# Scatter of the experts' results: two fp32r products with a 0-or-1 selection, the gate in VectorE's sum, and the next expert's turn between the two scatters

## Chip, core and metric

The kernel runs on one core of a Trainium2 chip. The metric is the device time in microseconds (us) of one execution. Three runs of the kernel before gave 2854.1 to 2858.06 us with a median of 2854.6.

## The reference

Two blocks of one model and two of another are computed one after the other for 256 tokens of 1024 features, all in fp32. The change touches only the mixture of experts in the second block. Eight experts exist, each token goes to two of them, and an expert is a SwiGLU with 3584 hidden columns:

```python
def _moe(x, w_router, w1, w3, w2):
    ...
    logits = (xt @ w_router).astype(jnp.float32)
    top_v, top_e = lax.top_k(logits, TOP_K)
    gates = jax.nn.softmax(top_v, axis=-1)
    ...
    def run(args):
        xb, e = args
        return _swiglu(xb, w1[e], w3[e], w2[e])
    yb = lax.map(run, (buf.reshape(n_blocks, EXPERT_BLOCK, D), block_e)).reshape(P, D)
    y = jnp.zeros((T, D), x.dtype).at[stok].add(yb[dest] * sg[:, None].astype(x.dtype))
```

The last line is the scatter: each expert's rows go back to their tokens, times the gate, and are summed.

## The kernel before, in words

**Products.** A weight product in fp32 accuracy is made from three fp32r products: each factor is split into a high and a low part, and `mm3` (lines L689, L690, L691) adds high x high, low x high and high x low. Weights come in units of 1 MB (4 x 128 rows by 512 columns). SyncE loads a unit into one of 5 `raw` buffers, ScalarE rounds it to `whi` (L1311), VectorE subtracts to `wlo` (L1717), both with 3 buffers, and TensorE takes 12 products from a unit of an expert. `Plan` writes one order of steps, and every engine walks through it (`Engine.run`). At each step an engine first prepares the weights of the units up to two ahead (`step` and `ahead`, `AHEAD = 2`), and then does its part of the step. So ScalarE and VectorE make the weights of unit u + 2 ahead of the evacuation of unit u's product, each in its own program order.

**An expert.** `select` (VectorE) makes from each token's place in the expert a matrix `sel` of 0 and 1 in fp32r, and `selg`, the same times the gate, in fp32. `gather` multiplies `sel` with the rows of x to give the expert's inputs `xT`, high and low. `turn` transposes `selg` on TensorE (L1005), and ScalarE copies it to `selgT` (L1411). Seven column blocks of e1 and e3 follow (28 units), each made into the hidden `hb` and transposed (`across`, L1015) into `hTe`. Then e2 runs in two column blocks of seven units. ScalarE copies each result to `hb` (L1522), and `scatter` multiplies `selgT` by it in fp32 (L1025). A plain fp32 product of 128x512 shows as two records in the trace. VectorE adds the result to `y` (L1830; for the very last one L2129, ahead of LayerNorm). Both scatters of an expert stand behind its last e2 unit, for the last expert the first one stands after three units of the second block.

**The branch.** The tokens of an expert fill one or two tiles of 128. The program holds both versions. `Engine.expert` reads the count and branches (L549: `If(self.count[ex] > 128)`), on TensorE, ScalarE and VectorE each. In these inputs every expert has one tile, so the second arm runs. TensorE does some things ahead of the branch: the `turn`, and nine products (three mm3) of the first unit (`open_expert`, L961). The branch stands behind them in its program. On ScalarE and VectorE the branch comes right after the last step of the expert before.

**Waits.** The sequencer of an engine takes instructions in order, and one that has to wait for a semaphore holds all behind it. Four PSUM buffers are given out in turn (`fill`), and each is free when its evacuation has been counted.

Of the kernel before, what the change touches and what calls it, by code (L numbers as in the profile page):

```python
# [70 lines left out]
class Memory:  # L71
# [21 lines left out]

    def new(self, name, shape, dt, c, side):
        self.serial += 1
        return c.enter_context(self.nc.sbuf_tensor(f"{name}_{self.serial}", shape, dt, side=side))
# [67 lines left out]
    def moe(self, t, hl, c):  # L164
        self.y1 = t("y", [128, 2, 1024], F32, c)
        with ExitStack() as c0:
# [10 lines left out]
            self.sel, self.selg = t("sel", [128, 2, 256], F32R, c0), t("selg", [128, 2, 256], F32, c0)  # L177
            self.selgT = t("selgT", [128, 2, 256], F32, c0)
# [72 lines left out]
class Plan:  # L251
# [128 lines left out]
    def moe(self):  # L380
        a, m, o = self.a, self.m, self.order
        for ex in range(8):
# [3 lines left out]
            o += [("begin", ex), ("turn", ex)]  # L386
# [14 lines left out]
            o += e2[0][ex == 7:] + e2[1][0:n] + [("scatter", ex, 0)] + e2[1][n:] + [("scatter", ex, 1), ("finish", ex)]  # L401
# [165 lines left out]
class Tensor(Engine):  # L567
# [25 lines left out]
    def do(self, step):  # L593
# [60 lines left out]
        elif what == "gather":  # L654
            self.gather(*a)
        elif what == "across":
# [297 lines left out]
    def expert(self, ex, j0, j1):  # L954

        self.turn(ex)
# [42 lines left out]
    def turn(self, ex):  # L999
        e, m = self.e, self.m  # L1000
        ps = self.fill(("turn", ex), ("selgT", ex))
        for s in range(2):
            for q in range(2):
                o = s * 256 + q * 128
                ins = e.transpose(ps[:, o:o + 128], m.selg[:, q, s * 128:s * 128 + 128], m.ident[:, :])  # L1005
# [12 lines left out]
    def scatter(self, ex, cb):  # L1018
        e, m = self.e, self.m
        ps = self.fill(("sc", ex, cb), ("y", ex, cb))  # L1020
        e.wait_ge(*self.at("selgT", ex))
        e.wait_ge(*self.at("ev", "e2", ex, cb))
        for q in range(2):
            for s in range(self.tiles):
                ins = e.matmul(ps[:, q * 512:q * 512 + 512], m.selgT[:, s, q * 128:q * 128 + 128], m.hb[:, cb, s, :],  # L1025
                               start=(s == 0), stop=(s == self.tiles - 1))
# [275 lines left out]
class Scalar(Engine):  # L1302
# [25 lines left out]
    def do(self, step):  # L1328
# [80 lines left out]
        elif what == "turn":  # L1409
            e.wait_ge(*self.at("full", "turn", a[0]))  # L1410
            e.activation(m.selgT[:, :, :], bands(self.psum("turn", a[0]), 4)[:, 0:2, :], ACT.Copy) \  # L1411
                .then_inc(*self.up("a_moe", ("selgT", a[0])))
        elif what == "across":
# [4 lines left out]
                .then_inc(*self.up("a_moe", ("hiT", "hTe", ex, cb)))  # L1418
        elif what == "rms":
# [45 lines left out]
    def product(self, g, G):  # L1465
# [47 lines left out]
        elif nm == "e1":  # L1513
# [3 lines left out]
            elif ex:  # L1517
                e.wait_ge(*self.at("full", "sc", ex - 1, cb))
# [183 lines left out]

    def copy(self, full, key, dst, o, n, parts=0):
# [6 lines left out]
class Vector(Engine):  # L1710
# [26 lines left out]
    def do(self, step):  # L1737
# [88 lines left out]
        elif what == "scatter" and a != (7, 1):  # L1826
# [3 lines left out]
            e.tensor_tensor(yy, yy, bands(self.psum("sc", *a)), ALU.add).then_inc(*self.up("d_moe", ("y",) + a))  # L1830
# [1072 lines left out]
```

## Time and profile before

| | |
|---|---|
| runs | 2854.6 us median, 2854.1 to 2858.06 |
| the profiled execution, its own time | 2857.58 us |
| its span, first to last instruction | 2855.5 us |
| mean granted TensorE clock | 0.986 of full speed |
| TensorE busy | 2743.5 us, 96% |
| VectorE busy | 2111.4 us, 74% |
| ScalarE busy | 1629.1 us, 57% |
| weight splitting on VectorE (L1717) | 1304.2 us in 588 instructions |

Engines are named PE (TensorE's products), PEld (its weight loads), DVE (VectorE), ACT (ScalarE), POOL and SP; a name with q is the engine's sequencer. Matmul records overlap, since a product is issued before the one ahead of it is through: the distance between two starts is what one costs in a row of them. The experts' stage lasts from about 845 to 1890 us of the span.

### The profile page before, as it was taken

How to read it: one execution, taken by the hardware profiler on the slowest of the kernel's cores; microseconds unless marked ns; L12 is line 12 of the kernel's file. 1: busy time of each engine (PE TensorE's matmuls, PEld its weight loads, DVE VectorE, ACT ScalarE, POOL GpSimd, SP SyncE). 2: the span in 40 equal slices, each digit the busy share in tenths (PEclk: the TensorE clock that was granted, in tenths of full speed). 3: DMA queues.
4: the chain of work that ended last, by engine and by line, in shares of the span. 5: the costliest groups of instructions: out<-in, count | busy, mean ns of one | idle time of the engine just before them, and what ended most of it. 6: DMA issues, size and time to landing. Idle time of an engine off the chain costs nothing.

```text
span 2855.5 us, 44738 instructions
## 1 busy us (share of the span) xinstructions
PE 2743.5 (96%) x19124; PEld 2324.9 (81%) x19124; DVE 2111.4 (74%) x2115; ACT 1629.1 (57%) x1630; POOL 140.4 (5%) x152
## 2 busy tenths in 40 slices
PE   7989999998999999999999999999899999998999
PEld 7867899887778787878788787878678988877997
DVE  6657655646769898988889898977756876766685
ACT  4345443454547676767667676755554654554563
POOL 1000000000000000000000000000330000052000
PEclk9999999999999999999999999999999999999999
DMA  7344655554349999999999999973205555322552
GB/s 215 118 134 139 194 188 172 150 169 152 122 163 350 322 357 332 340 350 338 343 346 340 324 355 347 361 238 130 79 30 174 178 192 168 124 70 69 175 181 104
DMA packets 360334, 616.16 MB, mean 216 GB/s; under 512 B 13776, under 2 KB 117200, under 8 KB 360112
## 3 DMA queue, kind: packets, MB, share of 16 engines
q1 hardware_dynamic: 355216, 598.61, 59.9%
q0 software_dynamic: 4896, 14.36, 2.2%
q8 instruction: 168, 2.75, 0.4%
q14 instruction: 54, 0.44, 0.0%
HBM read 611.88 MB, written 1.05 MB: 215 GB/s over the span
## 4 chain that ended last, share of the span: by engine, by line
PE 84%; DVE 8%; ACT 5%; issue 2%; DMA 0%; SPq 0%; DVEq 0%; ACTq 0%
PE ps L689 24%; PE ps L691 24%; PE ps L690 24%; ACT whi L1311 2%; DVE wlo L1717 2%; PE ps L1025 1%; PE ps L994 1%; PE ps L1171 1%; PE ps L1015 1%; PE ps L1150 1%; PE ps L1182 1%; PE ps L810 1%; ACT Q L1682 0%; PE ps L834 0%; ACT W L1706 0%
## 5 line engine op out<-in xcount | busy, mean ns | idle before, releaser
L1717 DVE TENSOR_TENSOR wlo<-raw,whi 128x2048 fp32r<-128x2048 f32 (+2 forms) x588 | 1304.2, 2223 | 426.0 <-ACT whi L1311 418.4
L1311 ACT ACTIVATE whi<-raw 128x2048 fp32r<-128x2048 f32 (+2 forms) x588 | 1092.9, 1860 | 422.9 <-PE ps L691 404.3
L689 PE MATMUL ps<-whi,xTh 128*128 128x512 f32 (+4 forms) x1464 | 582.4, 398 | 13.2 <-issue 5.9
L690 PE MATMUL ps<-wlo,xTh 128*128 128x512 f32 (+4 forms) x1464 | 571.4, 390 | 0.0
L691 PE MATMUL ps<-whi,xTl 128*128 128x512 f32 (+4 forms) x1464 | 570.7, 390 | 0.0
L689 PE MATMUL ps<-xTh,whi 128*128 128x256 f32 x1480 | 419.3, 283 | 0.0
L691 PE MATMUL ps<-xTh,wlo 128*128 128x256 f32 x1480 | 418.0, 282 | 0.0
L690 PE MATMUL ps<-xTl,whi 128*128 128x256 f32 x1480 | 418.0, 282 | 0.0
L689 PEld LDWEIGHTS ps<-whi,xTh 128*128 128x128 f32 x1464 | 280.7, 192 | 79.2 <-issue 13.5
L691 PEld LDWEIGHTS ps<-whi,xTl 128*128 128x128 f32 x1464 | 280.6, 192 | 62.1
L690 PEld LDWEIGHTS ps<-wlo,xTh 128*128 128x128 f32 x1464 | 281.2, 192 | 56.6
L689 PEld LDWEIGHTS ps<-xTh,whi 128*128 128x128 f32 x1480 | 279.7, 189 | 0.8 <-issue 0.7
L690 PEld LDWEIGHTS ps<-xTl,whi 128*128 128x128 f32 x1480 | 279.7, 189 | 0.1
L691 PEld LDWEIGHTS ps<-xTh,wlo 128*128 128x128 f32 x1480 | 279.5, 189 | 0.0
L689 PE MATMUL ps<-whi,hTeh 128*128 128x512 f32 x448 | 178.7, 399 | 0.0
L690 PE MATMUL ps<-wlo,hTeh 128*128 128x512 f32 x448 | 177.6, 396 | 0.0
L691 PE MATMUL ps<-whi,hTel 128*128 128x512 f32 x448 | 177.6, 396 | 0.0
L691 PEld LDWEIGHTS ps<-whi,hTel 128*128 128x128 f32 x448 | 84.4, 188 | 20.6
L689 PEld LDWEIGHTS ps<-whi,hTeh 128*128 128x128 f32 x448 | 84.4, 188 | 20.4 <-issue 0.2
L690 PEld LDWEIGHTS ps<-wlo,hTeh 128*128 128x128 f32 x448 | 84.4, 188 | 20.3 <-issue 0.2
L2584 DVE SCALAR_TENSOR_TENSOR co<-ci,cwf,co 128x256 f32<-128x256 f32 x176 | 73.8, 480 | 0.9
L689 PE MATMUL ps<-whi,hT2h 128*128 128x512 f32 x176 | 69.4, 395 | 0.0
(557 smaller groups left out, 3492.7 us busy)
## 6 DMA issues: line engine op xcount, KB each, us to landing
raw<-in_expert_w_dram SPq DMA_DIRECT2D x336, 1024.0 KB, 5.7
raw<-in_w_in_dram SPq DMA_DIRECT2D x76, 1024.0 KB, 5.1
raw<-in_w_up_dram SPq DMA_DIRECT2D x44, 1024.0 KB, 5.1
raw<-in_dense_w_dram SPq DMA_DIRECT2D x32, 1024.0 KB, 5.2
raw<-in_w_down_dram SPq DMA_DIRECT2D x20, 1024.0 KB, 5.4
raw<-in_w_out_dram SPq DMA_DIRECT2D x16, 1024.0 KB, 5.0
raw<-in_w_branch_diff_dram SPq DMA_DIRECT2D x8, 1024.0 KB, 5.0
raw<-in_w_ple_gate_dram SPq DMA_DIRECT2D x8, 1024.0 KB, 5.0
```

What stands on the lines that cost most here:

```text
L689: self.e.matmul(out, ah, bh, start=start, stop=False)
L690: self.e.matmul(out, ah, bl, start=False, stop=False)
L691: return self.e.matmul(out, al, bh, start=False, stop=stop)
L810: ins = self.e.transpose(ps[:, o:o + 128], src[:, t, (k0 + k) * 128:(k0 + k + 1) * 128], self.m.ident[:, :])
L994: ins = e.matmul(ps[:, d * 256:d * 256 + 256], m.xs[half][:, q, (d0 + d) * 128:(d0 + d + 1) * 128], m.sel[:, q, :], start=(q == 0), stop=( ...
L1015: ins = e.transpose(ps[:, o:o + 128], m.hb[:, cb % 2, t, k * 128:k * 128 + 128], m.ident[:, :])
L1025: ins = e.matmul(ps[:, q * 512:q * 512 + 512], m.selgT[:, s, q * 128:q * 128 + 128], m.hb[:, cb, s, :], start=(s == 0), stop=(s == self.ti ...
L1150: ins = self.e.transpose(out(r_), src[:, 128 * r_:128 * r_ + 128], self.m.ident[:, :])
L1171: ins = e.matmul(ps[half(a_), span(512 * c + 64 * r_)], m.E[d][r, s], TT[r, s], start=True, stop=True)
L1311: self.e.activation(self.m.hi[u % NHL][:, 0:n], self.m.raw[u % NRAW][:, 0:n], ACT.Copy) \
L1717: self.e.tensor_tensor(self.m.lo[u % NHL][:, 0:n], self.m.raw[u % NRAW][:, 0:n], self.m.hi[u % NHL][:, 0:n].bitcast(F32), ALU.subtract) \
L2584: ins = e.scalar_tensor_tensor(co[k][:, c, :], ci[:, c, tap:tap + 256], wc, co[k][:, c, :], ALU.mult, ALU.add)
```

## The change

`select` no longer makes `selg`. The turn now transposes `sel` itself, and the result is kept as `selT` in fp32r in two buffers, one expert apart. The results of e2 are split: ScalarE writes a high half (`expert_high`) and VectorE a low half (`expert_low`) in fp32r, into the part of `hTe` that e2 has read by then (`expert_sum`), no longer into `hb`. The scatter is then two fp32r products for each token tile, `selT` by high and `selT` by low. The gate is applied by VectorE when it adds to `y`. The halves of the first column block are made in a step of their own, `rest`, after two units of the second block. The turn of expert ex + 1 leaves `Tensor.expert` and becomes a step between the two scatters of expert ex; the one of expert 0 comes ahead of its `begin`, and the last expert has none behind it.

```diff
-            self.sel, self.selg = t("sel", [128, 2, 256], F32R, c0), t("selg", [128, 2, 256], F32, c0)
-            self.selgT = t("selgT", [128, 2, 256], F32, c0)
+            self.sel = t("sel", [128, 2, 256], F32R, c0)
+            self.selT = [t(f"selT{k}", [128, 2, 256], F32R, c0) for k in range(2)]
...
+    def expert_sum(self, cb):
+
+        return [h[:, 4 * cb:4 * cb + 4, :].rearrange("p (t a) n -> p t (a n)", t=2) for h in self.hTe]
...
-            o += [("begin", ex), ("turn", ex)]
+            o += [("turn", 0)] if ex == 0 else []
+            o += [("begin", ex)]
...
-            o += e2[0][ex == 7:] + e2[1][0:n] + [("scatter", ex, 0)] + e2[1][n:] + [("scatter", ex, 1), ("finish", ex)]
+            o += e2[0][ex == 7:] + e2[1][0:2] + [("rest", ex, 0)] + e2[1][2:n] + [("scatter", ex, 0)] + e2[1][n:]
+            o += [("turn", ex + 1)] if ex < 7 else []
+            o += [("scatter", ex, 1), ("finish", ex)]
...
     def expert(self, ex, j0, j1):
 
-        self.turn(ex)
         self.opened = ("e1", ex, 0)
...
     def turn(self, ex):
         e, m = self.e, self.m
-        ps = self.fill(("turn", ex), ("selgT", ex))
+        e.wait_ge(*self.at("sel", ex))
+        ps = self.fill(("turn", ex), ("selT", ex))
...
     def scatter(self, ex, cb):
         e, m = self.e, self.m
-        ps = self.fill(("sc", ex, cb), ("y", ex, cb))
-        e.wait_ge(*self.at("selgT", ex))
+        ps, T = self.fill(("sc", ex, cb), ("y", ex, cb)), m.selT[ex % 2]
+        high, low = m.expert_sum(cb)
+        e.wait_ge(*self.at("selT", ex))
+        e.wait_ge(*self.at("hiT", "ev", "e2", ex, cb))
+        for q in range(2):
+            for s in range(self.tiles):
+                e.matmul(ps[:, q * 512:q * 512 + 512], T[:, s, q * 128:q * 128 + 128], high[:, s, :], start=(s == 0), stop=False)
         e.wait_ge(*self.at("ev", "e2", ex, cb))
         for q in range(2):
             for s in range(self.tiles):
-                ins = e.matmul(ps[:, q * 512:q * 512 + 512], m.selgT[:, s, q * 128:q * 128 + 128], m.hb[:, cb, s, :],
-                               start=(s == 0), stop=(s == self.tiles - 1))
+                ins = e.matmul(ps[:, q * 512:q * 512 + 512], T[:, s, q * 128:q * 128 + 128], low[:, s, :], start=False,
+                               stop=(s == self.tiles - 1))
...
+        elif what == "rest":
+            e.wait_ge(*self.at("unit", self.p.unit[("e2", a[0], 1), 0]))
+            self.expert_high(*a)
...
         elif nm == "e2":
-            e.activation(m.hb[:, g[2], 0:self.tiles, :], bands(ps)[:, 0:self.tiles, :], ACT.Copy) \
-                .then_inc(*self.up("a_moe", ("ev",) + g))
+            if g[2]:
+                self.expert_high(*g[1:])
...
+    def expert_high(self, ex, cb):
+        g, n = ("e2", ex, cb), self.tiles
+        self.e.wait_ge(*self.at("full", *g))
+        self.e.activation(self.m.expert_sum(cb)[0][:, 0:n, :], bands(self.psum(*g))[:, 0:n, :], ACT.Copy) \
+            .then_inc(*self.up("a_moe", ("hiT", "ev") + g))
...
-            e.tensor_tensor(yy, yy, bands(self.psum("sc", *a)), ALU.add).then_inc(*self.up("d_moe", ("y",) + a))
+            for t in range(2):
+                ins = e.scalar_tensor_tensor(yy[:, t, :], bands(self.psum("sc", *a))[:, t, :], m.gate[:, t, a[0]:a[0] + 1],
+                                             yy[:, t, :], ALU.mult, ALU.add)
+            ins.then_inc(*self.up("d_moe", ("y",) + a))
...
+    def expert_low(self, ex, cb):
+        g, n, (high, low) = ("e2", ex, cb), self.tiles, self.m.expert_sum(cb)
+        self.e.wait_ge(*self.at("hiT", "ev", *g))
+        self.e.tensor_tensor(low[:, 0:n, :], bands(self.psum(*g))[:, 0:n, :], high[:, 0:n, :].bitcast(F32), ALU.subtract) \
+            .then_inc(*self.up("d_moe", ("ev",) + g))
...
         for t in range(2):
-            e.tensor_scalar(m.selg[:, t, :], m.iota[:, :], m.pos[:, t, ex:ex + 1], m.gate[:, t, ex:ex + 1], ALU.is_equal,
-                            ALU.mult)
             ins = e.tensor_scalar(m.sel[:, t, :], m.iota[:, :], m.pos[:, t, ex:ex + 1], m.mask[:, t, ex:ex + 1],
                                   ALU.is_equal, ALU.mult)
```

VectorE calls `expert_low` where ScalarE calls `expert_high`: in the step `rest`, and after the last unit of e2's second block. ScalarE's sigmoid of e1 waits for a transposition of the expert before instead of its scatter, and its copy of selT from expert 2 on also for the second scatter of two experts before.

## Rows read from the trace of the kernel before

**Rows 1.** The page, busy time of the engines.
```profile
PE 2743.5 (96%) x19124; PEld 2324.9 (81%) x19124; DVE 2111.4 (74%) x2115; ACT 1629.1 (57%) x1630; POOL 140.4 (5%) x152
```
**Rows 2.** Busy time by engine, from the scatter of one expert to the next.
```profile
core 0: us, PE busy (x) PEld busy (x) DVE busy (x) ACT busy (x) POOL busy (x), PEclk, DMA share, GB/s
1107.80:1236.70 128.90, 128.90 (x577) 103.36 (x576) 114.19 (x72) 91.00 (x61) 0.00 (x0) 1.00 0.96 343
```
**Rows 3.** Timeline of PE at the joint of the first two experts.
```profile
start us, us, engine line op out<-in xcount [idle before <-releaser]
...
977.43 3.60 PE L1025 MATMUL ps<-hb,selgT 128*128 128x512 f32 x8
980.87 0.60 PE L1005 MATMUL ps<-ident,selg 128*128 128x128 f32 x4
...
981.54 0.40 PE L690 MATMUL ps<-wlo,xTh 128*128 128x512 f32 x1
981.77 0.40 PE L691 MATMUL ps<-whi,xTl 128*128 128x512 f32 x1
...
984.89 0.50 PE L689 MATMUL ps<-whi,xTh 128*128 128x512 f32 x1 [1.31 <-issue]
```
**Rows 4.** Line L549 in the whole span: duration ns min/median/max, first and last start.
```profile
L549 PEldq COMPARE_BRANCH  x8: 3442/4606/5910, 851.0 to 1756.4; - x8
```
**Rows 5.** Lines L549 and L1022 at the joints of 977.43 and 1236.72.
```profile
L1022 PEldq EVENT_SEMAPHORE  x1: 51/51/51, 978.3 to 978.3; - x1
...
L549 PEldq COMPARE_BRANCH  x1: 5907/5907/5907, 978.9 to 978.9; - x1
...
L549 PEldq COMPARE_BRANCH  x1: 4438/4438/4438, 1238.0 to 1238.0; - x1
```
**Rows 6.** Timeline of PE at the joint of 1236.72.
```profile
1236.72 3.60 PE L1025 MATMUL ps<-hb,selgT 128*128 128x512 f32 x8
...
1242.70 0.39 PE L689 MATMUL ps<-whi,xTh 128*128 128x512 f32 x1
```
**Rows 7.** Waits of the experts' stage: us in total, times, longest.
```profile
PE ps L689 <- issue: 4.9, 4, 1.3
```
**Rows 8.** DMA within the branch, first of 978.9, then of 851.0.
```profile
q1 hardware_dynamic: 841, 1.66, 81.1%
q8 instruction: 2, 0.03, 4.0%
...
DMA packets 1, 0.02 MB, mean 5 GB/s; under 512 B 0, under 2 KB 0, under 8 KB 0
```
**Rows 9.** Timeline of ACT at the joint of 977.43.
```profile
977.63 0.60 ACT L1522 ACTIVATE hb<-ps 128x512 f32<-128x512 f32 x1 [0.84 <-PE ps L691]
```
**Rows 10.** Groups of VectorE and ScalarE by form in the experts' stage: busy, mean ns.
```profile
L1724 DVE TENSOR_TENSOR hTel<-ps,hTeh 128x512 fp32r<-128x512 f32 x56 | 38.2, 681 | 0.0
...
L1417 ACT ACTIVATE hTeh<-ps 128x512 fp32r<-128x512 f32 x56 | 33.3, 594 | 10.6 <-PE ps L1015 10.6
```
**Rows 11.** Timeline of DVE at the first joint, and at the last expert's end.
```profile
976.83 2.29 DVE L1717 TENSOR_TENSOR wlo<-raw,whi 128x2048 fp32r<-128x2048 f32 x1 [0.52 <-ACT whi L1311]
...
1881.18 2.29 DVE L1717 TENSOR_TENSOR wlo<-raw,whi 128x2048 fp32r<-128x2048 f32 x1 [0.51 <-ACT whi L1311]
```
**Rows 12.** Timeline of DVE ahead of the first expert.
```profile
848.39 2.35 DVE L1818 CAST xTl<-ps 128x1024 fp32r<-128x1024 f32 x2
```
**Rows 13.** Busy time in stretches with and behind idle times of PE.
```profile
536.80:538.60 1.80, 0.02 (x2) 0.04 (x1) 1.76 (x4) 0.01 (x1) 0.00 (x0) 1.00 0.00 0
539.80:543.10 3.30, 3.21 (x11) 3.19 (x11) 3.21 (x4) 1.71 (x3) 2.80 (x6) 0.50 0.71 114
984.90:990.00 5.10, 5.10 (x22) 4.13 (x23) 3.43 (x2) 3.21 (x3) 0.00 (x0) 1.00 0.57 192
2031.40:2038.10 6.70, 6.70 (x40) 4.51 (x40) 2.76 (x7) 4.06 (x9) 4.24 (x4) 0.50 0.67 241
```
**Rows 14.** Timeline of PE at the end of the last expert.
```profile
1882.72 1.96 PE L1025 MATMUL ps<-hb,selgT 128*128 128x512 f32 x4 [0.78 <-ACT hb L1522]
1884.51 10.46 PE L834 MATMUL ps<-ident 128*128 128x512 f32 x24
```

More of the change, by code:

```diff
@@ L655, in do @@
             self.gather(*a)
+        elif what == "turn":
+            self.turn(*a)
         elif what == "across":
@@ L1004, in turn @@
                 o = s * 256 + q * 128
-                ins = e.transpose(ps[:, o:o + 128], m.selg[:, q, s * 128:s * 128 + 128], m.ident[:, :])
+                ins = e.transpose(ps[:, o:o + 128], m.sel[:, q, s * 128:s * 128 + 128].bitcast(F32), m.ident[:, :])
         ins.then_inc(*self.up("turned_moe", ("full", "turn", ex)))
@@ L1410, in do @@
             e.wait_ge(*self.at("full", "turn", a[0]))
-            e.activation(m.selgT[:, :, :], bands(self.psum("turn", a[0]), 4)[:, 0:2, :], ACT.Copy) \
-                .then_inc(*self.up("a_moe", ("selgT", a[0])))
+            if a[0] > 1:
+                e.wait_ge(*self.at("full", "sc", a[0] - 2, 1))
+            e.activation(m.selT[a[0] % 2][:, :, :], bands(self.psum("turn", a[0]), 4)[:, 0:2, :], ACT.Copy) \
+                .then_inc(*self.up("a_moe", ("selT", a[0])))
         elif what == "across":
@@ L1517, in product @@
             elif ex:
-                e.wait_ge(*self.at("full", "sc", ex - 1, cb))
+                e.wait_ge(*self.at("full", "ac", ex - 1, 6 - cb))
             e.activation(m.hb[:, cb % 2, 0:self.tiles, :], bands(ps)[:, 0:self.tiles, :], ACT.Sigmoid) \
@@ L1829, in do @@
             e.wait_ge(*self.at("full", "sc", *a))
-            e.tensor_tensor(yy, yy, bands(self.psum("sc", *a)), ALU.add).then_inc(*self.up("d_moe", ("y",) + a))
+            for t in range(2):
+                ins = e.scalar_tensor_tensor(yy[:, t, :], bands(self.psum("sc", *a))[:, t, :], m.gate[:, t, a[0]:a[0] + 1],
+                                             yy[:, t, :], ALU.mult, ALU.add)
+            ins.then_inc(*self.up("d_moe", ("y",) + a))
+        elif what == "rest":
+            e.wait_ge(*self.at("unit", self.p.unit[("e2", a[0], 1), 0]))
+            self.expert_low(*a)
         elif what == "rms":
@@ L2128, in layernorm @@
                 e.wait_ge(*self.at("full", "sc", 7, 1, t))
-                e.tensor_tensor(yy, yy, bands(self.psum("sc", 7, 1))[:, t, :], ALU.add).then_inc(*self.up("d_moe", ("y", 7, 1)))
+                e.scalar_tensor_tensor(yy, bands(self.psum("sc", 7, 1))[:, t, :], m.gate[:, t, 7:8], yy, ALU.mult, ALU.add) \
+                    .then_inc(*self.up("d_moe", ("y", 7, 1)))
             e.wait_ge(*self.prev)
@@ L2181, in product @@
             return
-        if nm in ("q", "k", "v", "cq", "ck", "uq", "ukv", "pp", "rt", "e2", "dc", "gm", "qa", "ka"):
+        if nm in ("q", "k", "v", "cq", "ck", "uq", "ukv", "pp", "rt", "dc", "gm", "qa", "ka"):
             return
@@ L2256, in product @@
             return
+        elif nm == "e2":
+            if g[2]:
+                self.expert_low(*g[1:])
         elif nm == "oat":
```

## The prediction

> **What bounds the kernel now.** I read the page first. TensorE is busy for 96% of the span, VectorE for 74% [rows 1]. A change that takes work from TensorE could pay in full, unless that work covers something else. So I looked next at one expert. From the scatter of one to the scatter of the next are 128.9 us, all of it TensorE work at a granted clock of 1.00, with VectorE busy for 114 us and ScalarE for 91 [rows 2]. No product inside an expert waits for weights. The place that matters is the joint between two experts.
>
> In the timeline of a joint the scatter begins at 977.43. I call this moment t0. The eight records of the two fp32 scatters last to 980.87, 0.43 us each; four transposes (the turn) follow, then nine opening products of the next expert to about 983.4, and the tenth starts only at 984.89, after 1.31 us of idle time put down to "issue" [rows 3]. It waits for no engine. In program order the `If` of `Engine.expert` (L549) lies between the ninth product and the tenth. The row of L549 says what it costs TensorE's sequencer: 3.44 to 5.91 us, eight times [rows 4]. At this joint it starts at 978.9 and takes 5.9 us, so it ends at 984.8, and TensorE goes on at 984.89. At the joint of 1236.72 it takes 4.44 us from 1238.0, ends just as the nine products are spent, and the tenth follows at 1242.70 without a break [rows 5, 6]. So the sequencer runs ahead of the array and starts the branch while the scatter still runs; scatter, turn and nine products are its cover. Of the seven joints four have a branch of 4.4 to 4.6 us and resume at about t0 + 6.0; three have 5.8 to 5.9 us and resume at t0 + 7.2 to 7.5. These three and the first expert's are the four idle times of 4.9 us in sum in the stage's waits [rows 7]. The mean is t0 + 6.6. Within the branch the instruction queue reads 16 KB once or twice, next to a weight queue at 81% [rows 8]: the branch jumps over the arm for two tiles.
>
> The Trainium skill, page "Runtime: NRT & Kernel Launch", section "Instruction fetch mechanics", says that a taken branch whose target is outside a window of two pages must fetch the target page by DMA before execution can go on. The reads inside the branch agree with it. The page "Advanced Engine Details and Errata", section "Control Flow Timing", gives about 108 ns for a compare-and-branch. TensorE's 3.4 to 5.9 us disagree; by that figure the joints would be bound by the array alone, which is the third rival's case.
>
> What starts the branch? The sequencer passes its wait ahead of the second scatter (L1022) at 978.3 [rows 5], right after ScalarE's copy of the second e2 product ends (977.63 + 0.60) [rows 9]. The branch follows 0.6 us later. So it is this evacuation that sets its start, at t0 + 1.4 on the average, not the array.
>
> **The change part by part.**
>
> *The products.* A scatter with one tile is two fp32 products, each two records of 0.43 us. It becomes four fp32r products; the nearest row, fp32r with 512 columns, is issued 0.235 us after the one before [rows 3]. Two scatters fall from 3.44 to 1.88 us: 1.55 us of array time for each expert, 12.4 for eight.
>
> *The second scatter's wait.* It waited for one ScalarE copy. Now ScalarE writes the high half (0.59 us, as L1417) and then VectorE the low half (0.68, as L1724, the same size and types) [rows 10]. VectorE takes its steps in order, and its step for the last e2 unit begins with the low weights of the unit two ahead, the wlo of 976.83, which ends at 979.12 [rows 11]. The low half can only follow: ready at about 979.75, t0 + 2.3. The first scatter and the turn are over at t0 + 1.3, the second's high products at 1.8; then the array waits for some 0.6 us. Behind this wait stand two low products, the next expert's waits, nine opening products and the branch. The first expert shows this case: VectorE's xTl ended at about 850.75, the branch behind nine products started at 851.0 [rows 4, 12]. Between that 0.3 us and the 0.6 above I take 0.4: the branch starts at t0 + 2.7 instead of t0 + 1.4. The turn, moved forward, takes its four transposes out of the way from wait to branch, and its place in the cover with it.
>
> *Where TensorE resumes.* The array's own work would be done at t0 + 5.0 (2.4 + 0.47 + 2.1). The branch ends at 2.7 + its length, and 0.05 later work goes on. The median length of 4.6 gives t0 + 7.35, the mean of the seven, 5.1, gives 7.85; the shortest, 3.44, gives 6.2, the longest 8.65. I take 4.8, since the weight transfers that share the queues are a little nearer to their end: t0 + 7.55 against 6.6. That is 0.95 us later, seven times: +6.7. The ends are -0.4 and +2.05 each, so -3 and +14.
>
> *The clock.* An idle time of about 2.4 us now stands at each joint, with 0.6 us shortly before it. An idle time of 1.8 us was followed by a granted clock of 0.50 (1.2 instead of 2.4 GHz) for over 3 us; the joint's 1.3 us was followed by 1.00 [rows 3, 13]. The work in 3.4 us at half the clock costs 1.7 us more. I take four of the seven joints: +6.8. The bounds are 0 and, since a stretch of 6.7 us at 0.50 is in the rows too, 7 x 3.4 = 24.
>
> *The halves for cb 0 ("rest")* are made inside e2's second product. ScalarE idles for 0.8 to 0.9 us and VectorE for 0.5 ahead of each weight unit there [rows 9, 11], so 0.59 fits, and 0.68 makes one wlo 0.2 us late; the weights are prepared a unit ahead. Nothing; without that cover 0.2 x 8 = 1.6.
>
> *The rest of VectorE and ScalarE.* `select` loses two of its four instructions, the sum becomes two instructions of 512 columns for one of 1024, the low halves add 2 x 0.68: at most 1.4 us for an expert, on an engine that has 15 to spare [rows 2]. Nothing. After the joint, its next wlo would be ready at about t0 + 7.3 (sums to 5.0, then 2.29) and is needed some 3.5 us after TensorE resumes. selT is copied earlier than selgT was. Expert 0's turn stays where it was.
>
> *The last expert.* Its first scatter lies between weight units with no branch behind: four records go from 0.43 to 0.235 us, -0.8. Its second waited 0.78 us for ScalarE. Now the low half follows the wlo of 1881.18 (to 1883.45) [rows 11], is ready at 1884.1, and its products end at 1884.6, where the filler records began at 1884.51 before [rows 14]: +0.1. LayerNorm's chain on VectorE comes 0.7 us later, which these fillers (10.5 us, and nothing idle behind them) hide; else +0.7.
>
> *Sum*: 6.7 + 6.8 - 0.8 + 0.1 = +12.8. The profiled execution took 2857.58 us (span 2855.5), 3.0 above the median of the runs, 2854.6. On its own time that is 2870.4, on the median 2867.4.
>
> **Rivals.** *First: late branch, but the clock is kept, and branches are mostly short.* Then +4 to +8, less 0.7: 2858 to 2862. For it: a gap of 1.3 us left the clock alone. Against it: 2.4 is longer than the 1.8 that didn't.
>
> *Second: the branch is as quick as at the first expert*, where TensorE waited for VectorE right ahead of it too: 6.2 against 6.6, seven times, less 0.7: -3.5, 2851. Against it: one packet moved in that branch, the instruction read alone, while at a joint two weight loads are under way [rows 8].
>
> *Third, on the other side: the branch ends inside its cover.* It decides if the branch takes less than 2.3 us (5.0 less 2.7). The joint then goes from 6.6 to 5.0: 7 x -1.6 less 0.7 = -12, 2843. For it: twelve microseconds of array time do go, and TensorE is the busiest engine. Against it: the shortest of eight branches took 3.44.
>
> *Fourth: everything at its worst*, branches of 5.9 us and the clock down at each joint, twice as long at some: 14 + 12 to 24, 2880 to 2892. For it: three of seven were that long.
>
> VectorE as the bound has no chance of its own (115 of 129 us), and that fp32r saves nothing is excluded by its pitch.
>
> **How the numbers follow.** Forecast (2862 to 2877) 0.48; first rival 0.20; second 0.12; third 0.10; fourth 0.10. About 0.2%, 5.7 us, is what a measurement of this kernel can tell from no change. Faster beyond it: the third rival and a little of the second, 0.11. Slower: forecast, fourth, and nearly half of the first, 0.67. Same: 0.22. The range for 8 in 10 runs from 2851 to 2880; it leaves out the third and the fourth.
>
> **What would show it.** Right: the scatter's records 0.235 us apart; a wait of the second scatter's low products for VectorE until about t0 + 2.4; L549 on TensorE starting at t0 + 2.7 with 4 to 6 us; TensorE idle for 2 to 3.5 us behind the nine opening products, put down to "issue"; PEclk 0.50 behind several joints. Wrong: a low half ready by t0 + 1.5, ahead of the wlo; a branch of 2 us; or a branch that starts before the second scatter's wait is passed.

## The result, and the profile after

The change makes the kernel slower: 2887.86 us (median of four runs, 2881.13 to 2890.96) against 2855.63 us (2854.1 to 2858.06), a ratio of 1.0107 (95% interval 1.0094 to 1.0121). The direction and the place were forecast, the size was not: +32 us, where the forecast was +12.8 and its range ended at 2880. The profiled execution took 2886.58 us, 29.0 more than that of before.

The page of the kernel after, first the busy times that answer to [rows 1], then a line of its costliest groups. The last figures of that line are the idle time ahead of it and what ended it:
```profile
span 2884.5 us, 44791 instructions
...
PE 2746.4 (95%) x19124; PEld 2333.6 (81%) x19124; DVE 2121.5 (74%) x2130; ACT 1629.3 (56%) x1630; POOL 141.3 (5%) x152
...
L698 PE MATMUL ps<-whi,xTh 128*128 128x512 f32 (+4 forms) x1464 | 587.8, 402 | 33.6 <-issue 26.1
```
The span is 29 us longer and TensorE is busy for only 3 us more. The rest is idle time ahead of the first product of an `mm3` (L698, which was L689), and "issue" says that no engine released it. The waits of the experts' stage (850 to 1900 us), which answer to [rows 7]:
```profile
PE ps L698 <- issue: 25.1, 8, 3.6
PE ps L1039 <- DVE hTel L2301: 2.3, 7, 0.3
```
4.9 us of "issue" have become 25.1. The second scatter's wait for its low half is there at all seven joints with 0.3 us each.

Timeline of TensorE at the first joint, beside [rows 3]. L1035 is the scatter's high product, L1039 its low one, L1014 the turn:
```profile
977.64 0.63 PE L1035 MATMUL ps<-hTeh,selT 128*128 128x512 f32 x2
978.11 0.64 PE L1039 MATMUL ps<-hTel,selT 128*128 128x512 f32 x2
978.58 0.60 PE L1014 MATMUL ps<-ident,sel 128*128 128x128 f32 x4
978.94 0.71 PE L1035 MATMUL ps<-hTeh,selT 128*128 128x512 f32 x2
979.99 0.73 PE L1039 MATMUL ps<-hTel,selT 128*128 128x512 f32 x2 [0.34 <-DVE hTel L2301]
980.56 0.40 PE L698 MATMUL ps<-whi,xTh 128*128 128x512 f32 x1
...
982.43 0.40 PE L700 MATMUL ps<-whi,xTl 128*128 128x512 f32 x1
986.08 0.50 PE L698 MATMUL ps<-whi,xTh 128*128 128x512 f32 x1 [3.25 <-issue]
```
t0 is 977.64. The scatters are cheap as forecast, and the nine opening products are spent at 982.83. Then the array stands for 3.25 us. VectorE and ScalarE in the same stretch, beside [rows 9, 11], and the branch on TensorE's sequencer, L556 now, there and in the whole span, beside [rows 4, 5]:
```profile
977.04 2.29 DVE L1742 TENSOR_TENSOR wlo<-raw,whi 128x2048 fp32r<-128x2048 f32 x1 [0.52 <-ACT whi L1325]
979.25 0.68 DVE L2301 TENSOR_TENSOR hTel<-ps,hTeh 128x512 fp32r<-128x512 f32 x1
979.97 2.85 DVE L1856 SCALAR_TENSOR_TENSOR y<-ps,gate,y 128x512 f32<-128x512 f32 x4
```
```profile
977.90 0.60 ACT L1725 ACTIVATE hTeh<-ps 128x512 fp32r<-128x512 f32 x1 [0.90 <-PE ps L700]
```
```profile
L556 PEldq COMPARE_BRANCH  x1: 5674/5674/5674, 980.4 to 980.4; - x1
...
L556 PEldq COMPARE_BRANCH  x8: 3353/5820/6032, 851.3 to 1778.7; - x8
```
ScalarE has the high half at 978.50, but VectorE is in the wlo until 979.33, so the low half is ready at 979.93 and the branch starts at 980.4, t0 + 2.7. It is also longer: the median is 5.82 us, where [rows 4] had 4.61. Its end, 986.04, is where TensorE resumes.

What the branch waits for is seen in the queues. First SP's issue of a 1 MB weight load, before and after, then the DMA of the branch's first three microseconds (980.4 to 983.4) and of the rest (983.5 to 986; queue, kind: packets, MB, share):
```profile
979.15 0.37 SPq L2787 DMA_DIRECT2D raw<-in_expert_w_dram  x1
...
979.36 0.37 SPq L2826 DMA_DIRECT2D raw<-in_expert_w_dram  x1
```
```profile
DMA packets 546, 1.09 MB, mean 364 GB/s; under 512 B 16, under 2 KB 16, under 8 KB 545
q1 hardware_dynamic: 545, 1.08, 102.5%
q14 instruction: 1, 0.01, 0.6%
...
q1 hardware_dynamic: 59, 0.09, 9.4%
q8 instruction: 1, 0.02, 2.6%
```
The weights fill the DMA engines for three microseconds, and only then, at 983.55, comes q8, the read of 16 KB of instructions. The load was issued when the wlo of 977.04 was done, since that is what frees its buffer: 0.99 us ahead of the branch. In both kernels it comes at t0 + 1.72. It has not moved; the branch has moved from 0.2 to 0.4 us ahead of it to 1.0 us behind it. One read of 8 KB on the other instruction queue, q14, starts at 980.86, between the packets of two loads. By what rule the DMA engines serve their queues no run shows; what follows is about the times alone.

Last, busy time within the idle stretch, behind it, and over a mean period from this scatter on, beside [rows 2, 13] (PE, PEld, DVE, ACT, POOL, then PEclk, DMA share, GB/s):
```profile
982.90:986.00 3.10, 0.00 (x0) 0.00 (x0) 2.12 (x1) 0.00 (x0) 0.00 (x0) 1.00 0.31 114
987.00:990.00 3.00, 3.00 (x9) 2.32 (x8) 0.78 (x1) 1.91 (x1) 0.00 (x0) 0.50 0.83 315
...
977.64:1110.70 133.06, 129.47 (x578) 104.58 (x577) 115.44 (x74) 91.01 (x61) 0.00 (x0) 0.99 0.92 332
```
The stall comes at full clock, and 3.4 us at half of it follow, at every one of the seven joints. Taken from both traces, in us from t0 (means of the seven joints; the period, from one t0 to the next, is a mean of six):

| | before | after |
|---|---|---|
| branch starts | +1.3 to +1.5 | +2.70 to +2.74 |
| branch takes | 5.09 (4.41 to 5.91) | 5.83 (5.67 to 6.03) |
| instruction read starts, from the branch's start | 1.6 to 2.2, once 3.3 | 3.2 to 3.6 |
| TensorE resumes (start of the tenth product) | +6.58 | +8.60 |
| half clock behind it | none | 3.4 us, seven times |
| period | 129.60 | 133.06 |

So the seven joints cost 7 x 2.02 = 14.1 us of later resuming and 7 x (3.46 - 2.02) = 10.1 us of clock. The second figure is what is left of the longer period once the later resuming is taken off. With 0.6 us gained at the last expert and 0.2 lost ahead of the first joint that makes 23.8 of the 24.4 us by which the experts' stage grew.

### The profile page after: what moved, and what is told of

Read it like the earlier page. It is cut to its first block, busy times and chain, and to the rows that moved or that the text cites. A ratio compares the mean times of both kernels' runs of the same rounds, so it can differ in the third digit from the quotient of the medians.

```text
span 2884.5 us, 44791 instructions
## 1 busy us (share of the span) xinstructions
PE 2746.4 (95%) x19124; PEld 2333.6 (81%) x19124; DVE 2121.5 (74%) x2130; ACT 1629.3 (56%) x1630; POOL 141.3 (5%) x152
## 3 DMA queue, kind: packets, MB, share of 16 engines
HBM read 611.88 MB, written 1.05 MB: 212 GB/s over the span
## 4 chain that ended last, share of the span: by engine, by line
PE 82%; DVE 9%; ACT 6%; issue 3%; DMA 0%; DVEq 0%; SPq 0%; ACTq 0%
PE ps L698 24%; PE ps L700 24%; PE ps L699 23%; DVE wlo L1742 2%; ACT whi L1325 2%; PE ps L1002 1%; PE ps L1185 1%; PE ps L1024 1%; PE ps L1164 1%; PE ps L1196 1%; PE ps L819 1%; PE ps L843 0%; PE ps L932 0%; DMA raw<-in_w_in_dram 0%; ACT s L1621 0%
## 5 line engine op out<-in xcount | busy, mean ns | idle before, releaser
L698 PE MATMUL ps<-whi,xTh 128*128 128x512 f32 (+4 forms) x1464 | 587.8, 402 | 33.6 <-issue 26.1
L698 PE MATMUL ps<-xTh,whi 128*128 128x256 f32 x1480 | 418.9, 283 | 0.0
L698 PEld LDWEIGHTS ps<-whi,xTh 128*128 128x128 f32 x1464 | 284.4, 194 | 100.9 <-issue 34.2
L698 PEld LDWEIGHTS ps<-xTh,whi 128*128 128x128 f32 x1480 | 280.1, 189 | 0.8 <-issue 0.7
L698 PE MATMUL ps<-whi,hTeh 128*128 128x512 f32 x448 | 178.3, 398 | 0.0
L698 PEld LDWEIGHTS ps<-whi,hTeh 128*128 128x128 f32 x448 | 84.4, 188 | 20.2
L700 PE MATMUL ps<-whi,hT2l 128*128 128x512 f32 x176 | 69.5, 395 | 0.0
```

The source lines that it names most:

```text
L698: self.e.matmul(out, ah, bh, start=start, stop=False)
L700: return self.e.matmul(out, al, bh, start=False, stop=stop)
```

## The experiments

Two theories stood against each other at first. **The branch's cover**: everything is lost at the branch, because its start moved behind VectorE's wlo and its instruction read comes only behind the weight load that the same wlo releases. **The rest of the edit**: the split of e2's results, the sums, the turn's new place or the queues of ScalarE and VectorE cost something of their own. Each ratio is to the kernel before on the same chip; its medians there were 2856.5, 2857.2, 2857.3 and 2855.0 us for the four groups of runs below.

### No branch at all

Both kernels with only the arm for one tile, in all the engines that have it. What is left out is the arm for two tiles, which these inputs don't use.
```diff
-        with self.e.If(self.count[ex] > 128):
-            ...
-        with self.e.Else():
-            self.tiles = 1
-            for j in range(j0, j1):
-                self.step(j)
+        self.tiles = 1
+        for j in range(j0, j1):
+            self.step(j)
```


> The changed kernel without the branch: only the arm for one tile is in the program, which all eight experts of these inputs take; an expert of more than 128 tokens would be computed wrongly. Theory (the joint is bound by the branch, which starts late, and by the clock lost behind it): the tenth opening product follows the ninth without a break, resume at t0 + 5.0, no stretch at half clock in the experts' stage, expert period 133.1 -> about 129.1 us (the wait of 0.34 us for the low half stays), total 2887 -> about 2850. Rival (the halves, the sums or the weight pipeline cost the time): the period stays above 131 and the total above 2870.

> The kernel before without the branch, one-tile arm alone (it leaves out the arm for two tiles). Theory: the three joints that resume at t0 + 7.2 to 7.5 come down to 6.0, so -4 to -5 us in all, about 2850.5, period 128.8 everywhere. Against the changed kernel without the branch this gives what the fp32r scatter is worth by itself: 1.55 less 0.34 of waiting for the low half for each of seven joints, 0.8 in the last expert, so some 8 to 10 us if the array is the bound in both, and about 0 if fp32r saves nothing.

**Measured**: the kernel after takes 2844.96 us, ratio 0.9956 (0.9939 to 0.9972); the kernel before 2855.44, ratio 0.9995 (0.9983 to 1.0007). One period of each, after and then before:
```profile
1106.80:1234.60 127.80, 127.46 (x577) 103.33 (x577) 115.12 (x74) 91.00 (x61) 0.00 (x0) 1.00 0.97 345
```
```profile
1102.50:1231.30 128.80, 128.80 (x578) 103.46 (x577) 114.22 (x72) 90.98 (x61) 0.00 (x0) 1.00 0.95 342
```
Without the branch the edit does what it is made for: 1.0 us for each expert. From the first joint's t0 to the end of the last scatter the traces show 894.8 us against 902.1, so 7.4 less. The medians differ by 10.5, which their two intervals (together some 6 us either way) don't tell from that. The array's part of the prediction holds: 1.55 us less 0.58 of delay by the low half at each of seven joints, and 0.6 at the last expert, make 7.4. Both expected totals were missed. The kernel after came out 5 us below its 2850, with a period of 127.8 us where 129.1 was expected. The kernel before was to gain 4 to 5 us and shows no gain beyond its interval, though all its periods are 128.8 as expected. All that the kernel after loses, it loses at the branch: 2887.86 against 2844.96.

### The late copy alone

The kernel before, in which VectorE instead of ScalarE copies e2's second result, for experts 0 to 6. Nothing else of the change is in it.
```diff
         elif nm == "e2":
+            if g[2] and g[1] < 7: return                          # ScalarE
...
+        if nm == "e2" and g[2] and g[1] < 7:                      # VectorE
+            e.wait_ge(*self.at("full", *g))
+            e.tensor_copy(m.hb[:, 1, 0:self.tiles, :], ...).then_inc(...)
```


> The kernel before with one edit: VectorE instead of ScalarE copies e2's second result at the seven joints, so that it comes behind the wlo of the unit two ahead; products, gate and turn stay. Theory: the branch starts at t0 + 2.7 to 2.9 instead of 1.35, its instruction read falls behind the weight load issued at t0 + 1.7, it takes 5.7 to 6.0 us at all seven joints, TensorE resumes at t0 + 8.5 to 8.8 and the clock falls to 0.50 behind most joints (the array has 2.4 us more work after the wait here, so perhaps not behind all): 2869 to 2881. Rival (the branch's length was set by something else in the change, such as ScalarE's earlier branch): the branch starts late but takes 4.4 to 4.8 at most joints, resume at 7.3, +5 us, 2860.

**Measured**: 2883.34 us (2871.3 to 2891.12), ratio 1.0087 (1.0058 to 1.0116). VectorE and TensorE at the third joint:
```profile
1247.18 2.29 DVE L1719 TENSOR_TENSOR wlo<-raw,whi 128x2048 fp32r<-128x2048 f32 x1 [0.52 <-ACT whi L1311]
1249.39 0.68 DVE L2186 COPY hb<-ps 128x512 f32<-128x512 f32 x1
```
```profile
1250.22 1.95 PE L1025 MATMUL ps<-hb,selgT 128*128 128x512 f32 x4 [0.56 <-DVE hb L2186]
...
1256.39 0.51 PE L689 MATMUL ps<-whi,xTh 128*128 128x512 f32 x1 [1.67 <-issue]
```
```profile
L549 PEldq COMPARE_BRANCH  x1: 5627/5627/5627, 1250.7 to 1250.7; - x1
...
L549 PEldq COMPARE_BRANCH  x8: 3517/5875/7567, 853.7 to 1784.4; - x8
```
The copy stands behind the wlo, the branch starts at t0 + 2.8 to 3.0 and takes 5.6 to 6.2 us, at two joints with a second read 7.2 and 7.6. TensorE resumes at t0 + 8.6 to 10.6, and the half clock follows at five of seven joints. The median lies 2 us above the 2869 to 2881 expected. This one edit, without the new products, the gate in the sum or the moved turn, costs nearly what the whole change does.

### The whole change, but the load held back

The kernel after; SyncE waits with the load that the wlo releases until VectorE has added the second scatter, which is after the branch's start. The branch starts as late as before.
```diff
+            for ex in range(7):
+                if u == p.unit[("e2", ex, 1), 6] + 2 + NRAW:
+                    e.wait_ge(*self.at("y", ex, 1))
```


> The changed kernel with one wait more: at each joint SyncE issues the weight load that it issued at t0 + 1.7 only after the sum of the second scatter, at about t0 + 5.2. Theory (the instruction read of the branch stands in line behind that load): the branch still starts at t0 + 2.7 but takes 3.4 to 4.5 us, resume at t0 + 6.1 to 7.2, clock lost at half of the joints at most, total 2887 -> 2855 to 2868. Rival (the read is late for another reason, for example until the array has run dry): the branch keeps its 5.7 to 6.0 us and the total its 2887, or gets worse by the late load.

**Measured**: 2860.52 us (2853.69 to 2867.73), ratio 1.0009 (0.9999 to 1.002). The branch at the first joint and in the whole span, and the opening at that joint:
```profile
L556 PEldq COMPARE_BRANCH  x1: 3423/3423/3423, 983.5 to 983.5; - x1
...
L556 PEldq COMPARE_BRANCH  x8: 3407/3608/5114, 854.3 to 1763.2; - x8
```
```profile
983.16 0.74 PE L1039 MATMUL ps<-hTel,selT 128*128 128x512 f32 x2 [0.34 <-DVE hTel L2301]
...
987.00 0.50 PE L698 MATMUL ps<-whi,xTh 128*128 128x512 f32 x1 [1.01 <-issue]
```
The wait for the low half is the same 0.34 us and the branch starts at t0 + 2.70 as in the kernel after, but it takes 3.4 to 3.9 us instead of 5.7 to 6.0 (5.1 where two reads fall in it), TensorE idles for 1.0 to 1.5 us (2.7 at that one joint), and five of six periods are 129.1 to 129.5. Of what stands ahead of the branch only the load has moved. So the late start alone costs little; what costs is that it falls behind the load. The sixth period, 133.5 us, has a half clock of 6.8 us in it.

### Low half first

The kernel after; in the step of the last e2 unit VectorE makes the low half before the wlo instead of behind it.
```diff
+    def step(self, j):                                            # class Vector
+        s = self.p.order[j]
+        if s[0] == "u" and s[1][0] == "e2" and s[1][2] == 1 and s[2] == 6:
+            self.do(s)
+            self.j = j
+            self.ahead(min(self.p.end[j] + AHEAD, len(self.p.units)))
```


> The changed kernel with one turn of order: in the step of e2's last unit VectorE makes the low half first and the wlo of the unit two ahead after it. Theory: low half ready at t0 + 1.55, branch from t0 + 1.95, and the weight load that follows that wlo is issued at t0 + 3.9 instead of 1.7, behind the instruction read; the branch takes 3.4 to 4.6 us, resume at t0 + 5.4 to 6.6 against 6.55 before, clock kept; period 128 to 129.3, total 2850 to 2857. Rival (the weights made later at the joint cost what the earlier branch brings): TensorE waits for wlo behind the joint, total above 2860.

**Measured**: 2857.48 us (2854.0 to 2861.86), ratio 1.0001 (0.9991 to 1.0011).
```profile
L556 PEldq COMPARE_BRANCH  x8: 3347/3834/3966, 855.0 to 1756.1; - x8
```
The branch starts at t0 + 2.0, 3.1 us behind a load, and takes 3.6 to 4.0 us; TensorE resumes at t0 + 5.7 to 6.0, no half clock follows, and the periods are 128.6 to 128.9. The order of two VectorE instructions takes back the whole 30 us. From the first joint's t0 to the end of the last scatter it takes 900.9 us, where the kernel before takes 907.1 and the kernel after 931.2. And yet the total is the same as before. In its trace the stretch ahead of the first joint took 981.4 us against 977.4, with 6.8 us more at half clock, and the one behind the last scatter 977.5 against 970.9, with a wait of 1.5 us for VectorE (L836) that is new. These two stretches hardly differ between the programs, but over the fourteen traces of this document they lie between 972.8 and 981.4, and between 970.9 and 977.5. So a single trace can't say what takes the gain back, and it was not tried.

### A longer opening

The kernel after with 18 opening products instead of nine ahead of the branch, as cover.
```diff
-        for k in range(3):
-            self.mm3(...)
+        for j in range(2):
+            if j:
+                self.e.wait_ge(*self.at("lo", u + 1))
+            for k in range(3):
+                self.mm3(...)                                     # three of each unit
```


> The changed kernel with 18 opening products ahead of the branch instead of 9 (the first three k of the first two units). Theory: the branch starts at t0 + 2.8 to 3.0 and still takes 5.7 to 6.0 us, so it ends at 8.6 to 8.9, but the array works until t0 + 7.1 and has nine products less behind it; idle 1.5 us, which leaves the clock at 1.00; period about 129.7, total 2853 to 2862. It tells the two parts of the loss apart: 2.1 us of idle time and 1.4 us of clock for each joint. Rival: if the branch waited for the array to run dry it would now end at about t0 + 11 and the total would stay at 2885.

**Measured**: 2872.83 us (2867.05 to 2877.13), ratio 1.0056 (1.0034 to 1.0077). That is 15 us better than the kernel after, but the expected total was missed.
```profile
PE ps L698 <- issue: 16.1, 7, 6.9
PE ps L698 <- DVE wlo L1747: 4.4, 5, 0.9
...
L556 PEldq COMPARE_BRANCH  x8: 3338/5678/7312, 846.7 to 1766.5; - x8
```
The branch is as long as in the kernel after (5.6 to 6.2), so TensorE still resumes at t0 + 8.6 to 9.2. Nine more products, taken from behind the branch, cut the stall from 3.4 to 1.4 us at most joints, but 0.9 us come back at four of them, some 14 us behind t0. There TensorE waits for the fourth unit's wlo: the last three products of the first unit stand behind the branch now, and they free the buffers for it. At one joint two reads fall in the branch, it takes 7.3 us, and TensorE resumes only at t0 + 14.2. That is the 6.9 us of the first row. The branch explains 3 of them, and behind it the next 16 KB are read, 4.5 us after the load ahead of that read. Half clock follows at three joints.

### The rest of the edit

The kernel after, with e2's results in `hb`, no step `rest` and the scatter in fp32 as before, but with the 0-or-1 `selT` (in fp32), the gate in VectorE's sum and the turn between the scatters:
```diff
-            self.expert_high(*g[1:])
+            e.activation(m.hb[:, g[2], 0:self.tiles, :], ..., ACT.Copy).then_inc(...)
...
-   matmul(..., T, high, ...); matmul(..., T, low, ...)
+   matmul(..., T, m.hb[:, cb, s, :], ...)                        # fp32
```


> The changed kernel with the scatter put back to one fp32 product of ScalarE's copy in hb: the 0-or-1 selection, the gate in VectorE's sum and the turn between the scatters stay, the halves and the step rest go. Theory (these parts are harmless): branch from t0 + 1.35 with 4.4 to 5.9 us, same as the kernel before within 4 us, 2852 to 2860. Rival (the moved turn, or ScalarE's later branch behind it, does the harm): above 2865.

The kernel after with only the turn put back behind the second scatter:
```diff
-            o += [("turn", ex + 1)] if ex < 7 else []
             o += [("scatter", ex, 1)]
+            o += [("turn", ex + 1)] if ex < 7 else []
```


> The changed kernel with the turn behind both scatters again. Theory (the low half's wait starts the branch): it still starts at t0 + 2.7 to 2.8 and takes 5.7 to 6.0 us; the turn's 0.35 us moves into the cover where the array idles anyway, TensorE waits 0.35 longer for the low half, resume unchanged at t0 + 8.6, idle time a little shorter (3.3 instead of 3.65); total 2880 to 2888, as the changed kernel. Rival (the moved turn delays the branch or its read): the branch starts before t0 + 2.5 and the total falls by over 5 us.

**Measured**: with the fp32 scatter 2858.07 us, ratio 1.0004 (0.9994 to 1.0014); with the turn last 2885.73 us, ratio 1.0102 (1.0084 to 1.0121).
```profile
L556 PEldq COMPARE_BRANCH  x8: 3658/4496/6032, 849.0 to 1750.0; - x8
```
```profile
L557 PEldq COMPARE_BRANCH  x8: 3371/6004/6232, 846.7 to 1775.1; - x8
```
In the first the branch starts at t0 + 1.3 again, since ScalarE alone stands behind the second scatter, and it takes 4.3 to 4.8 us at six joints (6.0 at the seventh, where the read starts late). The gate in the sum, the selection and the moved turn are harmless. In the second the branch starts 0.1 to 0.2 us later than in the kernel after and takes 5.5 to 6.2 us, and TensorE idles for up to 0.6 us ahead of the low half's products instead of 0.34. So the place of the turn makes next to no difference.

### The load held back in the kernel before

The edit of SyncE above in the kernel before, where the wlo and so the load come behind the branch's start anyway.

> The kernel before with the weight load at each joint issued after the second sum (about t0 + 5) instead of t0 + 1.7. Theory (the read shares the queues with the loads in flight): the branch starts at t0 + 1.35 and takes 3.4 to 4.4 us at all joints, ending inside its cover; period 128.8, 4 to 5 us less in all, as without the branch: the same within noise or just faster. Rival (the two lengths 4.4 and 5.8 come from two instruction reads at once, not from the weight load): three joints still take 5.8 and resume at 7.2 to 7.5.

**Measured**: 2859.73 us (2854.86 to 2866.56), ratio 1.0017 (1.0006 to 1.0028).
```profile
L549 PEldq COMPARE_BRANCH  x8: 3670/4490/6075, 846.2 to 1750.8; - x8
```
The branches are 4.4 to 4.6 us long, with one of 6.08 whose read starts 3.6 us in. The expected 3.4 to 4.4 us were missed: the load that was held is issued behind the branch's start and does not set its length. The one issued 2.4 us ahead of it was not held. A later stall of 1.8 us, with half clock behind it, gives one period of 132.5. The kernel is slightly slower, which was not expected, and that period is the only new cost that its trace shows.

### The branch earlier, or the opening of one unit

Three more tries at a version that gains. In the first the second scatter comes behind `begin`, so the branch stands ahead of it and starts at t0 - 0.2. In the second, *low half first* with twelve opening products (the whole first unit). In the third, the first again with the load that would lie ahead of the branch held until the first scatter is done. The first and the third are right only where two neighbouring experts have the same number of tiles, as all have here.
```diff
-            o += [("begin", ex)]
+            o += [("begin", ex)] + ([("scatter", ex - 1, 1)] if ex else [])
...
+                if u == p.unit[("e2", ex, 1), 6] + 1 + NRAW:      # third only
+                    e.wait_ge(*self.at("full", "sc", ex, 0))
```


> The changed kernel with the second scatter of an expert moved behind the next expert's branch, as the first step of its arm (the scatter then uses the tile count of that arm, so it is right only where two neighbouring experts have the same number of tiles, as all have in these inputs). Theory: nothing ahead of the branch waits for the last e2 product any more, so the branch starts before t0 + 1 and ends inside first scatter, turn and nine products (to t0 + 3.4) or shortly after; the second scatter follows without waiting for the low half. Period 127.5 to 128 us, 7 x -1.9 less 0.8 against the kernel before: total 2840 to 2845. Rival (the branch's length grows when it starts among weight loads, to 6 us and more): resume at t0 + 5 to 6, period 129 to 130, no gain.

> The low half first, as in the run of that name, and twelve opening products instead of nine ahead of the branch. Theory: the branch ends at t0 + 5.6 to 6.0 as there and still bounds the joint, but three products fewer stand behind it: period 128.8 -> 128.1, 5 us less than the low half first alone, total about 2852. Rival (the first unit is released later by this, and the weights of the fourth unit come late): period stays at 128.8.

> The kernel of after_early_branch (second scatter behind the next branch, right where neighbouring experts have the same number of tiles), and the weight load that SyncE issued at t0 - 1.1, 0.88 us ahead of the branch, now waits for the first scatter (t0 + 1). The last load ahead of the branch is then 3.7 us old. Theory (in all runs the instruction read starts about 4.5 us after the last load issued ahead of the branch, or 0.9 to 1.0 us after the branch, whichever is later): read 0.9 to 1.3 us behind the branch, length 3.4 to 3.8, end at t0 + 3.2 to 3.6, where nine products and the first scatter end at 3.4; period 127.5 to 127.9, total 2838 to 2846, a version faster than both kernels. Rival (the read's start hangs on the branch's own place and not on the load): the branch keeps 5.9 to 6.3 us and the period its 130.3 or more.

**Measured**: the early branch 2876.53 us, ratio 1.0067 (1.005 to 1.0084); low half first with twelve products 2855.84 us, ratio 1.0002 (0.9989 to 1.0015); the early branch with the load held 2861.63 us, ratio 1.0024 (1.001 to 1.0038). The branches of the three:
```profile
L556 PEldq COMPARE_BRANCH  x8: 3475/6118/6354, 849.4 to 1766.1; - x8
```
```profile
L556 PEldq COMPARE_BRANCH  x8: 3387/3913/5419, 849.3 to 1752.8; - x8
```
```profile
L556 PEldq COMPARE_BRANCH  x8: 3267/3422/5107, 849.3 to 1756.4; - x8
```
The first misses its expected 2840 to 2845, but bears the theory out by another road: the branch starts nearly three microseconds earlier than in the kernel after and yet takes 5.9 to 6.4 us, more than there, because another load was issued 0.88 us ahead of it. The second missed its 2852 too: five periods are 128.3 as expected, but at two joints two reads fall in the branch (5.4 and 5.3 us), and behind one of these TensorE stands for another 3.0 us. The third takes the load ahead of the branch away, and the branch falls to 3.3 to 3.7 us at six joints (5.1 with two reads at the seventh); four periods are 127.8 to 128.0, as without any branch. But the total of 2838 to 2846 that was expected isn't reached. At two joints TensorE stands for about 5 us later, in the arm:
```profile
984.65 0.93 PE L1039 MATMUL ps<-hTel,selT 128*128 128x512 f32 x2 [4.84 <-issue]
...
PE ps L1039 <- issue: 10.1, 2, 5.3
...
q1 hardware_dynamic: 257, 0.52, 100.3%
q8 instruction: 1, 0.02, 4.3%
```
Here the next 16 KB of the arm's instructions are read (the last two rows, DMA at 981.9 to 983.3), and this read too starts only 4.7 us (5.5 at the other joint) after the last of two weight loads. No version with both arms beat the kernel before; only the one without the branch did.

## What set the branch's length

In nearly all branches of all runs the instruction read starts at the later of two times: about 1 us (0.8 to 1.3) after the branch, or about 4.5 us (mostly 4.2 to 4.8) after the last weight load issued ahead of the branch. From the traces, in us, with the length where one read falls in the branch:

| kernel | load to branch | branch to read | length |
|---|---|---|---|
| first expert (after) | 5.6 | 1.0 | 3.35 |
| load held | 3.8 | 0.9 to 1.3 | 3.4 to 3.9 |
| low half first | 3.1 | 1.2 to 1.6 | 3.6 to 4.0 |
| before | 2.4 | about 2.0 | 4.4 to 4.6 |
| late copy alone | 1.1 to 1.3 | 3.1 to 3.8 | 5.6 to 6.2 |
| after | 1.0 | 3.2 to 3.6 | 5.7 to 6.0 |
| early branch | 0.9 | 3.4 to 3.8 | 5.9 to 6.4 |

The length is the read's start plus 1.0 us for the read and some 1.4 us behind it. Where a second block is read within the branch, it takes 1.5 us more (two of the three long branches of the kernel before, 5.91 both).

## Why the prediction was right and wrong

- **What bounds the joint** was right: the branch on TensorE's sequencer, started by the wait ahead of the second scatter and not by the array.
- **The products** were right: the scatter costs what the fp32r pitch says, and without a branch the change gains 1.0 us for each expert.
- **The second scatter's wait** was right: branch at t0 + 2.7, as measured at all seven joints. The low half's products start 1.05 us after the high ones, which take 0.47: the delay of 0.58 us is the 0.6 that was given (the 0.34 in the row counts from the modelled end of the records). The turn and its cover come out as said.
- **Where TensorE resumes** is the step that failed. "I take 4.8, since the weight transfers that share the queues are a little nearer to their end" has the sign wrong. The prediction had the wlo that delays the low half, and it had the weight transfers next to the read, but it did not put the two together: the end of this wlo also frees a `raw` buffer, and SP issues 1 MB at once, 1 us ahead of the branch's new start. The transfers aren't nearer to their end, a new one has just begun. In place of the 4.8 us the seven branches took 5.83 on the average, and TensorE resumed 2.02 us later instead of 0.95, so +14.1 instead of +6.7. That is the upper end given there (+2.05 each, +14). *Load held* and *low half first* show the load as the cause: with one read the branch takes 3.4 to 4.0 us in both.
- **The clock** was mis-sized for the same reason: idle times of 3.2 to 3.6 us instead of 2.4, and a half clock behind seven of seven joints, not four. It costs 1.4 us at each instead of 1.7, so +10.1 instead of +6.8.
- **The edits costed at nothing** were free: `rest`, the sums and the selection show no new wait of TensorE in the stage, and the kernel with the fp32 scatter, which has all but the halves, runs like the kernel before.
- **The last expert** gained 0.6 us, given as 0.7.
- **The sum** for the experts' stage was +12.8 and is +24.4. Another 4.65 us of the profiled execution arise behind the experts, where the programs are equal. There the half clock lasts for 30.7 us instead of 28.8, which would be 1.0 us. The rest is no sign of the change: this stretch was 970.9 us in the trace of the kernel before and 975.6 in the kernel after, but 975.6 also in the kernel before without the branch. Single runs of the kernel before differ by up to 16.5 us on one chip. Why the medians differ by 32 us and not by 24 stays open.
- **The rivals**: the outcome lies where the fourth put it (5.9 us branches, clock down at every joint, 2880 to 2892), with a chance of 0.10; the second and the third needed a short branch. A quick one exists, at 3.4 us, but only when no load is ahead of it, so the second rival is what *load held* and *low half first* show.

The Trainium skill, page "Runtime: NRT & Kernel Launch", section "Instruction fetch mechanics", says that crossing into the next block of instructions is mostly hidden. At most joints the traces agree. At two joints of the early branch with the load held they don't, with 4.84 and 5.30 us, nor at single joints of other versions (3.0 us behind the branch in the one with twelve products).

**Left open.** Three single branches have one read that starts late though no load is nearer ahead of it than at the other joints: 5.77 us in the kernel before (read at 3.26), 6.08 us in its version with the load held (read at 3.6), 6.03 us with the fp32 scatter (read at 3.4). Why two reads fall in some branches is open too, and so is what takes back the gain of *low half first* outside the experts' stage.

## What to carry to other kernels

A taken branch to far code costs an instruction read, and here this read came only when the bulk load ahead of it was nearly through: look up what was issued in the last 4.5 us ahead of the branch, not only what covers it. When a wait is moved behind another instruction, ask what that instruction's end sets free besides the wait: here one wlo delayed the branch and released the transfer that the branch then waited for. An idle gap of a few microseconds on TensorE is to be counted with the half clock that may follow, here 1.4 us more for each.

## What the hardware showed beyond that

- The same branch takes 45 to 72 ns on ScalarE and VectorE and 3.3 to 7.6 us on TensorE.
- The clock did not fall in the gap but behind it: at 1.00 while TensorE stood for 3.25 us, then 3.4 us at 0.50 with TensorE busy. In the kernel after it followed each of seven gaps of 3.2 to 3.6 us, in *low half first* none of the seven of 1.1 to 1.5 us. In between the length of the gap alone did not decide: with the early branch the clock stayed at 1.00 behind gaps of 2.60, 2.38 and 2.25 us and fell behind one of 2.20.
